# Expert outputs stored by row and fetched per token, and gated-linear-attention levels computed for joined rows

## What is computed

```python
for l in range(DEPTH):
    x = layer_norm(ALPHA * x + hybrid_mixer(x, ...))
    x = layer_norm(ALPHA * x + memory_cross_attention(x, mem, ...))
    x = layer_norm(ALPHA * x + (swiglu(x, ...) if l % 2 == 0 else moe_swiglu(x, ...)))

def moe_swiglu(x, router, w13, w2):
    top_vals, top_idx = lax.top_k(x @ router, 2)
    gates = einsum(softmax(top_vals), one_hot(top_idx, 8))
    return sum(gates[..., e:e + 1] * swiglu(x, w13[e], w2[e]) for e in range(8))

# GLA: within a block, query i and key j <= i of the decays b (cumulated, one for each dimension d)
scores[i, j] = sum_d q[i, d] * k[j, d] * exp(b[i, d] - b[j, d])
```

## Time and profile before

| | |
|---|---|
| median of 3 runs | 1701.28 us (1699.81 to 1701.54) |
| the profiled execution | 1701.23 us |
| its span from the first instruction to the last | 1699.4 us |
| PE busy | 1666.1 us, 98% of the span |
| DVE busy | 1366.5 us, 80% |
| ACT busy | 1041.9 us, 61% |
| items of the experts | about 717 to 1684 us of the span |
| mixer, from scores to the end of GLA | 89 to 166 us (layer 0), 534 to 610 us (layer 1) |

### The profile page before, as it was taken

The page is one execution under the profiler, slowest core; times in us unless marked ns, Lnnn a source line. Parts: engine busy times, 40 slices in busy tenths (PEclk is TensorE's granted clock), DMA queues, the critical chain, the costliest instruction groups (busy, mean ns, idle before and its releaser), DMA issues.

```text
span 1699.4 us, 21961 instructions
## 1 busy us (share of the span) xinstructions
PE 1666.1 (98%) x8126; PEld 1379.5 (81%) x8126; DVE 1366.5 (80%) x1264; ACT 1041.9 (61%) x917; POOL 29.3 (2%) x37
## 2 busy tenths in 40 slices
PE   8999999999999999999999999999999999999996
PEld 7887888888887888878888888888888888888885
DVE  4788756545666886699899898898898998998997
ACT  4564444434345544377777777777777777777774
POOL 0001000000000100010000000000000000000000
PEclk9999999999999999999999999999999999999998
DMA  8523446546454545599999999999999999999992
GB/s 298 167 97 104 169 131 215 175 148 223 173 198 175 197 149 199 176 346 398 389 383 376 356 383 371 354 386 366 361 382 368 358 378 367 370 379 353 380 371 94
DMA packets 211001, 478.61 MB, mean 282 GB/s; under 512 B 14496, under 2 KB 17344, under 8 KB 210752
## 3 DMA queue, kind: packets, MB, share of 16 engines
q1 hardware_dynamic: 209952, 475.69, 77.1%
q0 software_dynamic: 576, 2.10, 0.3%
q10 hardware_dynamic: 416, 0.04, 0.0%
HBM read 474.65 MB, written 9.44 MB: 285 GB/s over the span
## 4 chain that ended last, share of the span: by engine, by line
PE 89%; DVE 8%; DMA 1%; issue 1%; ACT 1%; DVEq 0%; SPq 0%; ACTq 0%
PE ps L2357 51%; PE ps L1792 22%; PE ps L2212 4%; DVE w_lo L1102 2%; PE ps L1831 2%; PE ps L1835 2%; PE ps L2339 1%; PE ps L1752 1%; PE ps L2132 1%; PE ps L2113 1%; DVE qk L1348 1%; DVE ring_r L1090 1%; PE ps L1987 1%; DMA ring<-in_xa_wkv_dram 1%; DVE late L1242 1%
## 5 line engine op out<-in xcount | busy, mean ns | idle before, releaser
L1102 DVE TENSOR_TENSOR w_lo<-ring,w_hi 128x2048 fp32r<-128x2048 f32 x336 | 766.2, 2289 | 88.9 <-ACT w_hi L756 86.7
L756 ACT CAST w_hi<-ring 128x2048 fp32r<-128x2048 f32 x336 | 641.2, 1911 | 243.3 <-PE ps L2357 241.2
L2357 PE MATMUL ps<-w_hi,xe_hi 128*128 128x512 f32 x896 | 243.7, 394 | 0.2 <-DVE xe_lo L1599 0.2
L2357 PE MATMUL ps<-w_lo,xe_hi 128*128 128x512 f32 x896 | 240.4, 390 | 2.5 <-DVE w_lo L1102 2.5
L2357 PE MATMUL ps<-w_hi,xe_lo 128*128 128x512 f32 x896 | 239.9, 389 | 0.0
L2357 PEld LDWEIGHTS ps<-w_lo,xe_hi 128*128 128x128 f32 x896 | 167.7, 188 | 39.4 <-DVE w_lo L1102 4.8
L2357 PEld LDWEIGHTS ps<-w_hi,xe_lo 128*128 128x128 f32 x896 | 168.2, 188 | 35.8
L1792 PE MATMUL ps<-ring_r,xT_r 128*128 128x512 f32 (+1 forms) x736 | 193.9, 392 | 2.4 <-ACT ring_r L723 1.7
L2357 PEld LDWEIGHTS ps<-w_hi,xe_hi 128*128 128x128 f32 x896 | 165.2, 188 | 32.3 <-DVE xe_lo L1599 0.2
L1792 PEld LDWEIGHTS ps<-ring_r,xT_r 128*128 128x128 f32 x736 | 135.0, 188 | 34.2 <-ACT ring_r L723 2.2
L2357 PE MATMUL ps<-w_hi,he_hi 128*128 128x512 f32 x448 | 141.7, 397 | 0.0
(11 more groups left out here) (319 smaller groups left out, 1923.6 us busy)
## 6 DMA issues: line engine op xcount, KB each, us to landing
ring<-in_moe_w_dram SPq DMA_DIRECT2D x336, 1024.0 KB, 6.6
ring<-in_ffd_w_dram SPq DMA_DIRECT2D x31, 1024.0 KB, 5.0
ring<-in_w_in_dram SPq DMA_DIRECT2D x23, 1024.0 KB, 5.3
ring<-in_xa_wkv_dram SPq DMA_DIRECT2D x16, 1024.0 KB, 5.1
ring<-in_w_out_dram SPq DMA_DIRECT2D x8, 1024.0 KB, 5.0
ring<-in_xa_wq_dram SPq DMA_DIRECT2D x8, 1024.0 KB, 5.0
ring<-in_xa_wo_dram SPq DMA_DIRECT2D x8, 1024.0 KB, 5.0
sent_rows<-in_zeros_dram SPq DMA_DIRECT2D x12, 512.0 KB, 7.1
```

Source lines behind the costliest of these rows:

```text
L756: act.copy(w_hi[:, q % SPLIT_SLOTS, :], ring[:, RAW_ORDER[q % RAW_SLOTS], :]).then_inc(hi_ready, 1)
L1102: dve.tensor_tensor(w_lo[:, q % SPLIT_SLOTS, :], ring[:, RAW_ORDER[q % RAW_SLOTS], :], w_hi[:, q % SPLIT_SLOTS, :].bitcast(F32), ALU.subtr ...
L2357: ins = pe.matmul(ps[:, bank, :], xs[:, k, :], w[:, c, cols], start=(first and m == 0), stop=(last and m == 2))
```

## The change

**Experts.** y of an item is copied by ACT to `y_out` as it is, and SP stores it in block i of `sent_rows`, which the item's own input rows have left by then. No item but the last has `back`, `backT`, `y_lo`, scatter products or additions. The last item is written out apart from the loop. In it POOL fetches for each token the rows that its two experts gave (four indirect transfers, two at a time, into `xg` and `y_out`), and DVE adds them to `acc` with their gates at q = 20, 24, 28 and 32. The last item's own y goes the old way. `xg` and `y_out` now lie in the two tiles of `x`. The four transfers of `send_rows` no longer start together but with halves 13, 17, 21 and 25. **Mixer.** A level's product uses the two heads' partitions apart: eight matmuls over 64 partitions and 64 columns in place of four over 128 and 128. DVE computes the queries in one instruction and copies the scores in two. ACT takes over all pieces, the copy of heads A's output and its squares; the exponentials of the decays are cut in two. The gate's multiplication moves from POOL to DVE.

```diff
-SCATTERED_AT = [4, 5, 10, 11]
-ADDED_AT = [7, 8, 13, 14]
+COMBINED_AT = [20, 24, 28, 32]
+SENT_AT = [13, 17, 21, 25]
...
# SP
-                    if first and q == 24:
-                        sp.wait_ge(rows_out, 16 * 2 * T)
+                    if first and q == 34:
+                        sp.wait_ge(rows_moved, 16 * 2 * T)
+                        sp.wait_ge(acc_init, 1)
                         load_rows(1)
                     if not first and q == 12:
-                        sp.wait_ge(misc_ready[0], 5 * i + 1)
                         load_rows(i + 1)
+                    if not first and q == 14:
+                        sp.wait_ge(y_high, 2 * i)
+                        sp.dma_start(sent[i], y_out).then_inc(rows_stored, 16)
...
# POOL
+            def fetch_rows():
+
+                pool.wait_ge(fetch_ready, 1)
+                for n in range(2 * T):
+                    t, c = divmod(n, 2)
+                    if n >= 2:
+                        pool.wait_ge(rows_known, n)
+                    pool.indirect_dma_start((xg, y_out)[c], None, sent.rearrange("e p d -> (e p) d"),
+                                            bass.IndirectOffsetOnAxis(kept_i[:, c, t:t + 1], 0)).then_inc(rows_moved, 16)
...
# ACT
+                    if u == 4:
+                        act.wait_ge(pv_done, UNITS * l + 4)
+                        act.copy(o_tok[:, :, 0:S], ps[:, 0, :].rearrange("p (t n) -> p t n", t=T)).then_inc(oa_taken, 1)
                     if u + 1 < UNITS:
                         exps(u + 1)
...
+                    if final and q == 17:
+                        act.sem_inc(fetch_ready, 1)
                     high(q, i)
...
# DVE
-                    done(dve.tensor_scalar(rs[:, 1::2], rs[:, 1::2], lams[:, 3:4], None, ALU.mult))
...
-                        dve.wait_ge(pv_done, UNITS * l + 4)
-                        done(dve.tensor_copy(o_tok[:, :, 0:S], ps[:, 0, :].rearrange("p (t n) -> p t n", t=T)))
-                        dve.sem_inc(oa_taken, 1)
...
+            def combine_rows(n):
+
+                t, c = divmod(n, 2)
+                if c == 0:
+                    dve.wait_ge(rows_moved, 16 * (2 * T + n + 2))
+                dve.scalar_tensor_tensor(acc[:, t, :], (xg, y_out)[c], kept_w[:, c, t:t + 1], acc[:, t, :],
+                                         ALU.mult, ALU.add).then_inc(rows_known, 1)
...
-                    if not first and q == SPLIT_SLOTS - 1:
-                        take_y(i - 1)
-                    if not first and q in ADDED_AT:
-                        add_up(i - 1, ADDED_AT.index(q))
+                    if final and q in COMBINED_AT:
+                        combine_rows(COMBINED_AT.index(q))
...
# PE
-                            at = slice(b * P, (b + 1) * P)
-                            ins = pe.matmul(ps[:, level_bank(s), at], qk[:, s % 2, 1, at], qk[:, s % 2, 0, at],
-                                            start=True, stop=True)
+                            at, up = slice(b * P, (b + 1) * P), slice(b * (P // 2), (b + 1) * (P // 2))
+                            for hp in range(2):
+                                r = slice(64 * hp, 64 * hp + 64)
+                                ins = pe.matmul(ps[:, level_bank(s, hp), up], qk[r, s % 2, 1, at], qk[r, s % 2, 0, up],
+                                                start=True, stop=True)
...
-                    if q in SCATTERED_AT and not first:
-                        scatter(i - 1, SCATTERED_AT.index(q))
...
-                    if q == 33:
+                    if q == 33 and not final:
                         turn_rows(i, 7, 0)
-                    if q == 37:
+                    if q == 37 and not final:
                         turn_rows(i, 8, 1)
```

More of the change, by code:

```diff
@@ L1684, in add_up, with kept_rows, item @@
                     .then_inc(added[n], 1)
-            def item(i, first=False):
+            def kept_rows():
+                done(dve.tensor_scalar(row_step[:, 0, 0:1], table[:, 4:5], float(P), None, ALU.mult))
+                kf, rf = (v.rearrange("p c t -> p (c t)") for v in (kept[:, :, :], row_of[:, :, :]))
+                done(dve.tensor_scalar(kf, rf, row_step[:, 0, 0:1], None, ALU.is_lt))
+                done(dve.tensor_tensor(kept_w[:, :, :], kept[:, :, :], rmx[:, 0:2, :], ALU.mult))
+                done(dve.scalar_tensor_tensor(kept[:, :, :], row_of[:, :, :], float(P), kept[:, :, :], ALU.add, ALU.mult))
+                done(dve.tensor_copy(kept_i[:, :, :], kept[:, :, :]))
+            def combine_rows(n):
[4 more added lines that the diff above has]
+                                         ALU.mult, ALU.add).then_inc(rows_known, 1)
+            def item(i, first=False, final=False):
                 for q in range(SPLIT_SLOTS if first else 0, ITEM_HALVES):
@@ L1718, in item @@
                                  MOE_PAIRS * i + (n + 1))
-                    if q in GATHERED_AT:
+                    if q in GATHERED_AT and not final:
                         g = GATHERED_AT.index(q)
@@ L1723, in _ @@
             item(0, first=True)
-            n_items = dve.value_load(table_i[0:1, 0:1], min_val=NE, max_val=NE + EXTRA)
             last = dve.value_load(table_i[0:1, 4:5], min_val=NE - 1, max_val=NE + EXTRA - 1)
-            with dve.Fori(1, n_items) as i:
+            with dve.Fori(1, last) as i:
                 item(i)
+            item(last, final=True)
             take_y(last)
@@ L2081, in _ @@
                         v0 = C_VAL + CV * hd
-                        ins = pe.matmul(o, st[:, 2 * pair + t, hp, :], h[:, t, v0:v0 + CV], start=True, stop=(t == 0))
+                        ins = pe.matmul(o, st[:, hp, 2 * pair + t, :], h[:, t, v0:v0 + CV], start=True, stop=(t == 0))
                         if t == 1:
@@ L2085, in _ @@
                     ins.then_inc(gla_out, 1)
-                piece(l, 7, range(1, 6))
+                piece(l, 7, range(0, 5))
                 for t in range(T):
@@ L2090, in _ @@
                     turn_tile(TURN["mix", l], o_tok, t)
-                piece(l, 7, range(6, 8))
+                piece(l, 7, range(5, 8))
                 turned(TURN["mix", l], 0)
@@ L2427, in item @@
                         ins.then_inc(misc_ready[b], 1)
-                for b in range(2):
-                    pe.wait_ge(misc_taken[b], 5 * i + (6 - b))
+                if not final:
+                    for b in range(2):
+                        pe.wait_ge(misc_taken[b], MISC_USES[b] * i + (6 - b))
             item(0, first=True)
-            n_items = pe.value_load(table_i[0:1, 0:1], min_val=NE, max_val=NE + EXTRA)
             last = pe.value_load(table_i[0:1, 4:5], min_val=NE - 1, max_val=NE + EXTRA - 1)
-            with pe.Fori(1, n_items) as i:
+            with pe.Fori(1, last) as i:
                 item(i)
+            item(last, final=True)
             for n in range(2):
                 for t in range(T):
-                    scatter(last, 2 * t + n, last_banks=True)
+                    scatter(last, 2 * t + n)
 _INS = ["x", "mem", "positions", "w_in", "lam_q1", "lam_k1", "lam_q2", "lam_k2", "diff_norm_g", "gla_wa2", "gla_ba",
```

175 lines of the change are left out of this document (88 added, 87 removed).

## The result

The changed kernel took 1676.77 us (median of 4 runs, 1675.66 to 1677.05), beside 1700.55 us for the kernel before in the same comparison: ratio 0.9859, 95% interval 0.9843 to 0.9875. That is 23.8 us faster by the medians. Its profiled execution has a span of 1675.2 us, 24.2 less than before. Timed once more beside other kernels it gave 1676.61 against 1699.33 us (0.9866, 0.9851 to 0.9881). The forecast was 1679.7 us.

The account below looks back on a forecast made before the run. PE bounds the items and waits at places for DVE in the mixer; items 15.1, attention 3.6, GLA 2.6, clock 0.8, less 0.6 stall, make 21.5 us off 1701.23: 1679.7 us, range 1674.5 to 1689.

Parts of the forecast that it names:

- Items: Experts' items: removed scatter products and transposes come off PE, which is never idle there; 15.1 us gained.
- Transfers: Experts' items: the added store of 0.52 MB an item stays hidden, with traffic rising from 370 to 381 GB/s.
- rival (d): Transfers become the bound in the items; at a 370 GB/s ceiling 1705 us, slower than before below about 375; chance 0.04.
- Sends and kept rows: Item 0: SP may stand 0 to 3.5 us for the sends, kept-rows instructions cost 0 to 1 us; both taken as 0.
- Last item: Gathers for DVE's additions: some 2 us late costs nothing; 0.6 us of stall taken in all, bounds 0 and 10.
- Rival (b): Last item: gathers land 5 us or more too late in both rounds; 1690 us; chance 0.11.
- Attention: Mixer: PE's 1.34 us wait before u = 4's value products and 0.5 us for `difference` go; 1.8 us a layer.
- GLA: Mixer: PE's 4.0 us of waiting for DVE goes, less dearer level products and a new wait; 1.3 us a layer.
- one query instruction fewer takes off 0.43: GLA levels: with 0.1 added for a second masked copy, DVE saves 0.33 us a level and no longer limits PE.
- The new wait for `stx`: GLA output products: PE idles 0.5 us while ACT copies the sixth piece and then `stx`.
- the level product: GLA: sixteen instructions over 64 partitions take 1.09 us against 0.81, read as a time for each instruction.
- Clock: Layer 0, attention: the fall of the granted clock costs up to 1.7 us; half taken, 0.8 us gained.

Follow-up runs that it names:

- the halves apart: The kernel before with only the changed experts' part, and with only the changed mixer: 14.2 and 8.0 us faster than the kernel before, sum 22.2 us.
- store_x4: The changed kernel with each item's output stored four times, three into rows nobody reads: 1677.10 us, against 1676.61 for the changed kernel beside it.
- copy_on_dve: The changed kernel with the copy of heads A's output back on DVE: 1678.60 us, ratio 0.9878 to the kernel before.
- items_only: The kernel before with the experts' part of the changed one, mixer as before: 1685.39 us against 1699.55, ratio 0.9916.
- fetch_late: The changed kernel with the last item's signal for the gathers given at ACT's q = 22 instead of 17: 1685.91 us, 9.3 us slower than the changed kernel.
- levels_only: The kernel before with the new levels of GLA and nothing else: 1695.04 us against 1698.95, ratio 0.9975.
- levels_old: The changed kernel with the levels of GLA put back as before: 1678.04 us, ratio 0.9877 to the kernel before.
- clear_early: The changed kernel with the twelve zero transfers issued in layer 0's dense part, not at layer 1's start: 1675.01 us against 1698.95 before, ratio 0.9856.

## Why the prediction was right, and where it was not

It forecast 21.5 us off; the medians gave 23.8 and 22.7, the halves apart 22.2. That it came so near is in part luck, since its errors have both signs. Against the 24.2 us of the two traces the items gave 0.7 us less than forecast, attention 0.3 and GLA 0.5 more, the clock in layer 0 0.8 more, the starts of the layers 2.6 that were not forecast, and the rest took back 0.7.

**Items.** 15.1 - 0.6 us forecast, 13.8 measured, and no stall in the last item, so the 0.6 was not due. The removed products are right in size. What was missed is a small loss behind each group of transposes. Before and after, from one group to the next, with 48 products between them:

```profile
1139.14 0.60 PE L2339 MATMUL ps<-square,hge 128*128 128x128 f32 x4
...
1142.32 1.07 PE L2357 MATMUL ps<-w_hi,xe_hi 128*128 128x512 f32 x4
...
1150.49 0.60 PE L2339 MATMUL ps<-square,hge 128*128 128x128 f32 x4
```

```profile
1123.25 0.60 PE L2369 MATMUL ps<-square,hge 128*128 128x128 f32 x4
...
1126.46 1.07 PE L2387 MATMUL ps<-w_hi,xe_hi 128*128 128x512 f32 x4
...
1134.63 0.60 PE L2369 MATMUL ps<-square,hge 128*128 128x128 f32 x4
```

11.35 against 11.38 us; over seven groups 11.353 and 11.375. The matmuls are not slower as such: the last 36 products take 8.17 us in both. The transposes and the twelve products behind them take 3.21 us and not 3.18. An item is 10.5 such distances long, so 0.23 us an item, 1.8 in all: 15.1 - 1.8 = 13.3, near the 13.8. All kernels with the new experts' part have it, those with the old part do not, and four times the store does not add to it. What causes it stays open.

**Transfers.** The store was hidden, as forecast, and `store_x4` shows the cover: rival (d) was far off. The prediction set the 358 GB/s of the Trainium skill (DMA: Bandwidth & Descriptors, Where 436 GB/s comes from) against its rows, and the 380 and 393 GB/s over 121 us lie above it too. One figure of rival (d) was miscounted: slower than before begins where seven items are 6.4 us longer, at 45.1 MB in 121.3 us, 372 GB/s and not 375.

**Sends and kept rows.** Nothing forecast, nothing seen: SP stood 2.6 us for the sends, and no engine waited for it.

**Last item.** The DVE wait was 0 and not up to 2 us; the slack was 2.6 us against 2. Rival (b) needed gathers 5 us late; they were early by 3 us in the first pair, and just in time in the second.

**Attention.** 1.8 us a layer forecast, 1.9 and 2.0 measured. The cause is wider than given: about half of the wait went without the copy's move, as `copy_on_dve` shows.

**GLA.** 1.3 us a layer forecast, 1.4 and 1.7 measured, but the reason failed. The step "one query instruction fewer takes off 0.43 ... DVE is then no longer behind PE's steps" is true, and yet not what the gain hangs on: the kernel with the old levels has nearly the whole of it. On top of the other edits the levels are worth 0.2 us. (The prediction's sum also takes off 0.6 for a wait that it puts at 0.5.) The new wait for `stx` came as forecast, 0.5 us, and the level product cost 1.04 us against 1.09, for another reason than the one given: the row it was read from also alternates the halves (and their banks).

**Clock.** 0.8 us forecast for layer 0, half of a fall. The two traces showed 1.6 there, and a second fall at the start of layer 1 that was not in the sum. How often a fall comes varies between executions, so the medians hold less of it than the trace.

## What to carry to other kernels

When two edits relieve the same engine, measure each alone and each removed: here either one brought most of the gain, and the second was worth 0.2 us a layer more. Look in a slow stretch for what is queued ahead of the transfer that is waited for; issuing twelve unhurried transfers some 250 us earlier was worth 1.45 us, more than the rewritten level products brought on top of the other edits. A difference of two profiled executions also holds the clock's falls of each, so subtract those before putting a gain down to an edit.

## What the runs showed of the hardware that was not expected

- Eight products over 64 partitions and 64 columns (sixteen instructions) take 1.04 us when the two halves of the partitions, each with its own bank of PSUM, alternate, and 1.54 us when they come one after the other.
- The granted clock fell from 1.00 to 0.50 at waits of PE of 1.35 and 2.36 us (before), of 1.34, 2.30 and 1.37 us (`items_only`) and of 6.42 us (`fetch_late`), and did not at 1.33 us in both layers (`levels_only`), 1.34 us (layer 1, before) and 2.2 us (`levels_old`). A wait of one or two microseconds may cost its length again, or nothing.
- DMA carried 393 GB/s over 121 us in the items with PE busy throughout (`store_x4`); in the last item, where ACT then waited for weights 16 times, PE did not feel it.
- A 1 MB transfer issued behind three of 512 KB from HBM to HBM landed 10.1 and 9.0 us after its issue, and 5.1 us without them (before, changed kernel, `clear_early`).
- In every kernel with the new experts' part the first twelve 512-column matmuls behind a group of transposes took some 0.02 us longer together, at the same granted clock of 1.00; the 36 behind them took the same 8.17 us.
